# Projection of a hybrid layer: linear attention's levels in pairs, ten steps a chunk, queries scaled behind the eviction

## The chip, the cores and the metric

One core of one Trainium2 chip. The metric is the device time of one execution in microseconds (us). Engines: PE is TensorE (matmuls), PEld its weight loads, DVE is VectorE, ACT is ScalarE, POOL is GpSimd, SP is SyncE, which issues nearly all transfers. Each engine runs its own list of instructions in order, and semaphores order them against each other.

## What is computed

One decoder layer over 2048 prompt tokens and 8 x 8 sample tokens. Cut to what matters here:

```python
h = rms_norm(x, g_norm)
z = h @ w_in                       # the projection: 17 blocks of 512 columns
# forgetting attention on qa, ka, va; short convolution on xc, bc, cc, gc
# gated linear attention (GLA), 4 heads, key 64, value 128:
a = log_sigmoid(lrb @ w_gla_up + b_gla) / 16
b = cumsum(a)                      # within a chunk
att[t, s] = sum_d q[t, d] * k[s, d] * exp(b[t, d] - b[s, d])     # s <= t
o = (q * exp(b)) @ state + att @ v
state = exp(b_last) * state + (k * exp(b_last - b)).T @ v
out = x + merge(branches) @ w_out
```

The kernel computes this in four phases: the projection with GLA, the convolution and the forget sums woven into it (0 to about 1677 us of the span), attention of the prompt, attention of the samples, and merge with output projection.

## The kernel before

**Units.** The projection's matmuls are cut into 481 units. Units 17 to 480 go through 8 pairs of column blocks `j`; each pair takes 7 products `f` of sums and differences of operand blocks (so that 7 products do the work of 8), and each product takes 8 units `tp` of 12 matmuls of 128x512 into one of 3 buffers `z_ps`. After the 8 units of f = 0 and f = 4 comes one unit `sa` of 16 matmuls for the samples. PE starts unit u when unit u - 3 is evicted.

**What DVE does at unit u**, in this order: `split` (L1147: the low half of a weight slice for the next product, behind ACT's high half L969; at tp 2, 4, 6 and 7, L1147 is awaited by PE in the next product), `gla_steps(u)`, `product(u - 2)` (L1187, L1192, L1194; only for the blocks of j = 2 and 3), `evict(u)` (L1168 to L1175: one instruction, two for f = 5; f = 0 is evicted by ACT, L985). ACT: `split`, its GLA steps, `evict(u)`, the three activations of `sigmoid(u - 1)` (L1007 to L1011). POOL: `weight_sum` (L542 to L560), its GLA steps, one step of `convolve` (L568 to L574), none of which is tied to a unit's end except by data. PE: the unit, then its GLA step. SP: the loads of operands and weights, stores, its GLA step.

**GLA.** 16 prompt chunks of 128 tokens and one chunk of the 64 sample tokens (c = 16). Masks split the triangle of a chunk into 7 levels (3 for c = 16). For level i: POOL writes `dist` (L589, `distance`), ACT takes it to `dec` in two activations (L1044, L1049), DVE writes `qE` = queries times `dec` (L1266, two instructions), POOL writes `kE` (L597, `scale_keys`), PE multiplies them into `a_ps` (L1504, 4 matmuls, signals `paired`), DVE copies the level's blocks under a mask into `att` (L1213, `keep`, signals `kept`). `dist`, `dec`, `qE`, `kE` and `a_ps` have two buffers each, level n in buffer n % 2. PE's level n waits for `kept` of level n - 1.

**Steps.** `CHUNK_STEP` puts the steps of a chunk on units. `OPEN` lists the units of tp 0 to 6 from unit 52 on, without `sa`; a chunk takes 20 of them. Before, step s of chunk c lies at place 5 + 20c + 20s // 14 of that list, so steps are one or two places apart. Step -3: SP loads q, k, v. Step 0: PE turns them. Step 1: ACT and DVE make logits, the diagonal and the sum `cum` (about ten instructions). Step s has DVE's `qE` of level s - 2, PE's matmuls of level s - 3, DVE's `keep` of level s - 4. Step 9: `exp_b`, `q_in` (L1274), `k_out` (L1279). Step 10: PE turns `k_out`. Step 11: output matmuls (L1520, L1523), ACT copies `k_tok`. Step 12: `grow` (L1547). Step 13: `update` (L1220, four instructions) of the state. For c = 16, steps 12 to 19 take one sample each on PE (L1536, 8 matmuls; then, behind `wait_from(pe, state_ready, LAST + n)`, `grow`, 4 matmuls), and DVE's `update` of sample n is step 13 + n.

Of the kernel before, what the change touches and what calls it, by code (L numbers as in the profile page):

```python
# [163 lines left out]
def project(nc, arena, x_all, g_norm, w_main, w_tail, h_ops, z, tail_t, kv_out, g_gla, conv_w, state_conv, ext_prompt, ext_sample,  # L164
# [9 lines left out]
    LAST = TILES - 1  # L174
# [112 lines left out]
    PERIOD, BEHIND = 20, 5  # L287
    CHUNK_STEP = {}
    for c in range(TILES):
        for step in range(-3, 14 if c < LAST else 14 + DEC_BATCH):  # L290
            CHUNK_STEP.setdefault(OPEN[BEHIND + PERIOD * c + PERIOD * step // 14], []).append((c, step))
# [12 lines left out]
    with ExitStack() as stack:  # L304
# [182 lines left out]

        def level(c, i):
            return LEVELS * c + i
# [22 lines left out]
        def _(pool):  # L512
# [116 lines left out]
            for u in range(len(UNITS)):  # L629
# [6 lines left out]
                for c, step in CHUNK_STEP.get(u, []):  # L636
                    i = step - 2
                    if 0 <= i < len(halves_of(c)):
                        distance(c, i)
                        scale_keys(c, i)  # L640
                    elif step == 9:
                        distance(c, len(halves_of(c)))
# [5 lines left out]
        def _(sp):  # L648
# [142 lines left out]
            def gla(c, step):  # L791
                if step == -3:
# [11 lines left out]
                if step == (12 if c < LAST else 12 + DEC_BATCH):  # L804
# [14 lines left out]
                if c == LAST and step >= 14:  # L819
                    n = step - 14  # L820
# [103 lines left out]
        def _(act):  # L924
# [94 lines left out]
            def gla(c, step):  # L1019
                i = step - 2  # L1020
# [20 lines left out]
                elif 0 <= i < len(halves_of(c)):  # L1041
# [8 lines left out]
                elif step == 9:  # L1050
# [8 lines left out]
                elif step == 11:  # L1059
# [3 lines left out]
                if step == (12 if c < LAST else 12 + DEC_BATCH):  # L1063
# [55 lines left out]
        def _(dve):  # L1119
# [86 lines left out]
            def keep(c, i):  # L1206
                n = level(c, i)
                h = halves_of(c)[i]
                dve.wait_ge(paired, n + 1)
# [15 lines left out]
            def gla(c, step):  # L1225
                i = step - 2
# [31 lines left out]
                if 0 <= i - 2 < len(halves_of(c)):  # L1258
                    keep(c, i - 2)
                if 0 <= i < len(halves_of(c)):  # L1260
# [9 lines left out]
                elif step == 9:  # L1270
# [9 lines left out]
                if c < LAST and step == 13:  # L1280
# [3 lines left out]
                if c == LAST and 13 <= step < 13 + DEC_BATCH:  # L1284
                    n = step - 13
                    dve.wait_ge(grown, LAST + n + 1)
                    update(s_state[:, n], exp_b[:, :, (n + 1) * DEC_SEQ - 1])
                if c == LAST and 11 <= step < 11 + DEC_BATCH:
                    n = step - 11
# [53 lines left out]
            for u in range(len(UNITS) + 3):  # L1343
# [21 lines left out]
                gla_steps(u)  # L1365
# [3 lines left out]
                if u < len(UNITS):  # L1369
                    evict(u)  # L1370
                if u < TILES:
# [6 lines left out]
        def _(pe):  # L1378
# [106 lines left out]
            def gla(c, step):  # L1485
                i = step - 3
# [10 lines left out]
                elif 0 <= i < len(halves_of(c)):  # L1497
# [4 lines left out]
                    wait_from(pe, kept, n)  # L1502
# [4 lines left out]
                elif step == 10:  # L1507
# [6 lines left out]
                elif step == 11:  # L1514
# [12 lines left out]
                if c < LAST and step == 12:  # L1527
# [1718 lines left out]
```

## Time and profile before

| what | us |
|---|---|
| median of 3 runs (3643.61 to 3645.72) | 3643.92 |
| the profiled execution | 3641.52 |
| its span, first to last instruction | 3639.8 |
| PE busy in the span | 3415.4 (94%) |
| DVE, ACT, POOL busy in the span | 2193.9, 1797.8, 1653.6 |

The profile is of one execution. A row of a timeline is one instruction or a few equal ones (x4); what stands in square brackets is how long the engine had been idle and what it waited for. The spans of PE's matmuls are modelled and overlap: what counts is the distance of their starts.

### The profile page before, as it was taken

The page shows a single profiled execution, that of the slowest core. Times are in us where ns is not written, and L with a number is a line of the kernel's source. Part 1 is how long each engine was busy: PE and PEld are TensorE (multiplying, and loading weights), DVE is VectorE, ACT ScalarE, POOL GpSimd, SP SyncE. Part 2 cuts the span into 40 slices and gives each one's busy share as a digit, 9 for nine tenths or more (in the row PEclk, how much of TensorE's full clock was granted, in tenths as well). Part 3 has the DMA queues.
Part 4 walks back from the last instruction along what each step waited for, and adds up shares of the span by engine and source line. Part 5 has one row for each costly group of instructions (what it writes and reads, how often), then busy time and mean ns, then how long its engine had stood idle before and what let it go on. Part 6 is the DMA issues. An engine that isn't in the chain of part 4 may idle for free. (4 is left out here: it accounts for less than half of the span.)

```text
span 3639.8 us, 55125 instructions
## 1 busy us (share of the span) xinstructions
PE 3415.4 (94%) x17143; PEld 2675.7 (74%) x17143; DVE 2193.9 (60%) x3609; ACT 1797.8 (49%) x3707; POOL 1653.6 (45%) x1238
## 2 busy tenths in 40 slices
PE   7899999999999999997998998999999999899999
PEld 6678888777787778885666665777777776688787
DVE  4425456767665655554766663788888887544432
ACT  4411222544424464635676676777777776311222
POOL 1411314153535452211777775777777777222100
PEclk9999999999999999997999999999999999999999
DMA  7878787877888887885011113999999999544322
GB/s 269 321 231 287 211 281 235 300 254 247 277 304 295 269 264 239 260 233 167 13 36 47 30 42 109 318 331 333 331 330 336 334 333 314 194 159 159 136 93 78
DMA packets 430936, 818.82 MB, mean 225 GB/s; under 512 B 98449, under 2 KB 119865, under 8 KB 430670
## 3 DMA queue, kind: packets, MB, share of 16 engines
q1 hardware_dynamic: 418518, 808.32, 66.9%
q10 hardware_dynamic: 11584, 5.13, 0.5%
q8 instruction: 142, 2.33, 0.3%
q0 software_dynamic: 576, 2.10, 0.2%
q14 instruction: 116, 0.95, 0.1%
HBM read 674.12 MB, written 141.32 MB: 224 GB/s over the span
## 5 line engine op out<-in xcount | busy, mean ns | idle before, releaser
L1460 PE MATMUL prj_z_ps<-prj_w_hi,prj_h_ring 128*128 128x512 f32 x1792 | 725.7, 405 | 11.8 <-DMA prj_h_ring<-hops_scratch 7.2
L2381 POOL TENSOR_TENSOR sa_v_lo<-sa_v_raw,sa_v_hi 128x1024 fp32r<-128x1024 f32 x256 | 608.6, 2400 | 218.3 <-DVE sa_v_hi L2520 217.8
L1462 PE MATMUL prj_z_ps<-prj_w_hi,prj_h_ring 128*128 128x512 f32 x1792 | 704.9, 393 | 0.0
L1461 PE MATMUL prj_z_ps<-prj_w_lo,prj_h_ring 128*128 128x512 f32 x1792 | 703.3, 392 | 0.0
L1877 POOL TENSOR_TENSOR pa_p_lo<-pa_probs,pa_p_hi 128x512 fp32r<-128x512 f32 (+1 forms) x320 | 367.2, 1162 | 161.7 <-ACT pa_p_hi L1890 144.8
L2514 DVE TENSOR_TENSOR sa_kT_lo<-sa_t_ps,sa_kT_hi 128x512 fp32r<-128x512 f32 x512 | 345.3, 686 | 138.2 <-ACT sa_kT_hi L2403 134.9
L1460 PEld LDWEIGHTS prj_z_ps<-prj_w_hi,prj_h_ring 128*128 128x128 f32 x1792 | 340.4, 190 | 80.1 <-issue 8.0
L1462 PEld LDWEIGHTS prj_z_ps<-prj_w_hi,prj_h_ring 128*128 128x128 f32 x1792 | 339.3, 189 | 75.3
L1461 PEld LDWEIGHTS prj_z_ps<-prj_w_lo,prj_h_ring 128*128 128x128 f32 x1792 | 340.6, 190 | 66.7
L2403 ACT CAST sa_kT_hi<-sa_t_ps 128x512 fp32r<-128x512 f32 x512 | 291.6, 590 | 126.2 <-PE sa_t_ps L2667 119.1
L2667 PE MATMUL sa_t_ps<-arena_ident,arena_k_raw 128*128 128x128 f32 x2048 | 301.3, 278 | 26.7 <-DVE sa_kT_lo L2514 18.3
L2667 PEld LDWEIGHTS sa_t_ps<-arena_ident,arena_k_raw 128*128 128x128 f32 x2048 | 241.2, 141 | 107.3 <-DVE sa_kT_lo L2514 33.5
L589 POOL TENSOR_TENSOR prj_dist<-prj_cum 128x256 f32<-128x256 f32 x132 | 98.4, 746 | 380.5 <-DVE prj_cum L1256 380.5
L1919 ACT ACTIVATE pa_probs<-pa_st_ps 128x512 f32<-128x512 f32 (+1 forms) x320 | 171.1, 535 | 149.6 <-PE pa_st_ps L2124 72.6
L2014 DVE TENSOR_REDUCE pa_part_max<-pa_max_ps 128x1 f32<-128x512 f32 (+2 forms) x320 | 182.8, 603 | 103.1 <-PE pa_max_ps L2102 83.4
L1175 DVE TENSOR_TENSOR prj_z_sb<-prj_z_ps,prj_xy 128x512 f32<-128x512 f32 x192 | 132.3, 689 | 185.1 <-PE prj_z_ps L1462 183.9
L2730 PE MATMUL sa_o_ps<-sa_v_hi,sa_p_both 128*128 128x512 f32 x512 | 215.0, 420 | 9.0 <-POOL sa_v_lo L2381 5.9
L2673 PE MATMUL sa_s_ps<-sa_kT_hi,sa_q_both 128*128 128x512 f32 x512 | 212.6, 415 | 0.0
L597 POOL TENSOR_TENSOR prj_kE<-prj_kT,prj_dec 128x256 f32<-128x256 f32 x115 | 90.8, 790 | 254.6 <-ACT prj_dec L1049 197.3
L2731 PE MATMUL sa_o_ps<-sa_v_lo,sa_p_both 128*64 128x512 f32 x512 | 203.7, 398 | 0.0
L2674 PE MATMUL sa_s_ps<-sa_kT_lo,sa_q_both 128*64 128x512 f32 x512 | 202.2, 395 | 0.0
L2850 POOL TENSOR_TENSOR mo_merged<-mo_merged,arena_mg 128x1024 f32<-128x1024 f32 x34 | 81.8, 2406 | 243.6 <-DVE arena_mg L3052 243.6
(422 smaller groups left out, 7349.6 us busy)
## 6 DMA issues: line engine op xcount, KB each, us to landing
prj_h_ring<-hops_scratch SPq DMA_DIRECT2D x448, 512.0 KB, 4.6
arena_k_raw<-in_cache_k_dram SPq DMA_DIRECT2D x512, 256.0 KB, 4.1
sa_v_raw<-in_cache_v_dram SPq DMA_DIRECT2D x512, 256.0 KB, 4.3
z_scratch<-prj_z_sb SPq DMA_DIRECT2D x256, 256.0 KB, 5.4
prj_raw<-in_w_main_dram SPq DMA_DIRECT2D x104, 256.0 KB, 5.9
arena_mg<-z_scratch SPq DMA_DIRECT2D x51, 512.0 KB, 4.7
hops_scratch<-prj_h_ring SPq DMA_DIRECT2D x32, 512.0 KB, 5.8
arena_cu<-extp_scratch SPq DMA_DIRECT2D x48, 256.0 KB
```

The lines of the kernel that those rows point to most:

```text
L1460: pe.matmul(out, h[:, 0, k], hi, start=(k == 0), stop=False)
L1461: pe.matmul(out, h[:, 0, k], lo, start=False, stop=False)
L1462: mm = pe.matmul(out, h[:, 1, k], hi, start=False, stop=(k == HK - 1))
L1877: pool.tensor_tensor(p_lo[:, s % P_RING, 0:w], probs[:, s % P_RING, 0:w], p_hi[:, s % P_RING, 0:w].bitcast(F32), ALU.subtract).then_inc(pl ...
L2381: pool.tensor_tensor(v_lo[:, w % 2, at], v_raw[:, w % RING, at], v_hi[:, w % 2, at].bitcast(F32), ALU.subtract).then_inc(vlo_ready, 1)
L2403: act.copy(kT_hi[:, g % 2, :, j * PAGE:(j + 1) * PAGE], heads_of(t_ps[:, j % 2])).then_inc(khi_ready, 1)
L2514: dve.tensor_tensor(kT_lo[:, g % 2, :, at], heads_of(t_ps[:, j % 2]), kT_hi[:, g % 2, :, at].bitcast(F32), ALU.subtract).then_inc(klo_read ...
L2667: mm = pe.transpose(t_ps[:, j % 2, pair * PAGE:(pair + 1) * PAGE], k_raw[:, g % RING, j, pair * P:(pair + 1) * P], ident[:])
L2673: pe.matmul(out, q, hi(pair), start=(pair == 0), stop=False, skip_group_check=True)
L2674: mm = pe.matmul(out[0:R], q[:, 0:R], lo(pair), start=False, stop=(pair == PAIRS - 1), skip_group_check=True)
L2730: pe.matmul(out, p_both[:, slot, j], v_hi[:, slot, j], start=begin, stop=False, skip_group_check=True)
L2731: mm = pe.matmul(out[0:R], p_both[:, slot, j, 0:R], v_lo[:, slot, j], start=False, stop=end, skip_group_check=True)
```

## The change

Levels 2i and 2i + 1 share one step. A chunk has ten steps (0 to 9) that lie exactly two places of `OPEN` apart, and the loads step -2. The new helper `levels_at(c, step, lag)` gives the two levels of a step; DVE's `qE` has lag 2, PE's matmuls lag 3, `keep` lag 4. DVE calls `keep` right behind the splits of a unit and all its other GLA work behind `evict(u)`. PE's two levels of a step wait for `kept` of all levels before them, `keep` waits for `paired` of both levels of its step. `exp_b`, `q_in`, `k_out` come at step 5, the turn of `k_out` at 6, `k_tok` at 7, output matmuls and `grow` at 8, the `update` at 9. For c = 16, PE takes sample n at step 9 + n and DVE's `update` of sample n is step 10 + n; the last step is 18 (unit 479, before it was unit 473).

```diff
-    PERIOD, BEHIND = 20, 5
+    PERIOD, BEHIND, STEPS = 20, 5, 10
-        for step in range(-3, 14 if c < LAST else 14 + DEC_BATCH):
-            CHUNK_STEP.setdefault(OPEN[BEHIND + PERIOD * c + PERIOD * step // 14], []).append((c, step))
+        for step in range(-2, STEPS if c < LAST else 11 + DEC_BATCH):
+            CHUNK_STEP.setdefault(OPEN[BEHIND + PERIOD * c + PERIOD // STEPS * step], []).append((c, step))
...
+        def levels_at(c, step, lag):
+            return [i for i in (2 * (step - lag), 2 * (step - lag) + 1) if 0 <= i < len(halves_of(c))]
...
-                    i = step - 2
-                    if 0 <= i < len(halves_of(c)):
+                    for i in levels_at(c, step, 2):
                         distance(c, i)
+                    for i in levels_at(c, step, 2):
                         scale_keys(c, i)
-                    elif step == 9:
+                    if step == 5:
                         distance(c, len(halves_of(c)))
...
             def gla(c, step):
-                if step == -3:
+                if step == -2:
...
-                if step == (12 if c < LAST else 12 + DEC_BATCH):
+                if step == (9 if c < LAST else 9 + DEC_BATCH):
                     sp.wait_ge(o_ready, c + 1)
...
-                elif 0 <= i < len(halves_of(c)):
+                for i in levels_at(c, step, 2):
                     n = turn_of_dec(c, i)
                     act.wait_ge(apart, n + 1)
...
-                dve.wait_ge(paired, n + 1)
+                dve.wait_ge(paired, level(c, min(i // 2 * 2 + 2, len(halves_of(c)))))
...
-                if 0 <= i - 2 < len(halves_of(c)):
-                    keep(c, i - 2)
-                if 0 <= i < len(halves_of(c)):
+                for i in levels_at(c, step, 2):
                     n, h = level(c, i), halves_of(c)[i]
                     dve.wait_ge(dec_ready, turn_of_dec(c, i) + 1)
...
-                if c < LAST and step == 13:
+                if c < LAST and step == 9:
                     dve.wait_ge(grown, c + 1)
...
-                if c == LAST and 13 <= step < 13 + DEC_BATCH:
-                    n = step - 13
+                if c == LAST and 10 <= step < 10 + DEC_BATCH:
+                    n = step - 10
                     dve.wait_ge(grown, LAST + n + 1)
                     update(s_state[:, n], exp_b[:, :, (n + 1) * DEC_SEQ - 1])
...
-                gla_steps(u)
+                for c, step in CHUNK_STEP.get(u, []):
+                    for i in levels_at(c, step, 4):
+                        keep(c, i)
                 if u in FORGET_STEP:
                     forget(FORGET_STEP[u])
                 product(u - 2)
                 if u < len(UNITS):
                     evict(u)
+                gla_steps(u)
...
-                elif 0 <= i < len(halves_of(c)):
+                for i in levels_at(c, step, 3):
...
-                    wait_from(pe, kept, n)
+                    wait_from(pe, kept, level(c, i // 2 * 2))
...
-                elif step == 10:
+                if step == 6:
...
-                elif step == 11:
+                elif step == 8:
...
-                if c < LAST and step == 12:
+                if c < LAST and step == 8:
                     pe.wait_ge(ktok_ready, c + 1)
                     grow(k_tok[:], c)
-                if c == LAST and 12 <= step < 12 + DEC_BATCH:
-                    n = step - 12
+                if c == LAST and 9 <= step < 9 + DEC_BATCH:
+                    n = step - 9
```

## Rows read from the trace of the kernel before

**Rows 1.** Windows of the projection: length, busy PE, PEld, DVE, ACT, POOL, clock, DMA.
```profile
880.00:909.00 29.00, 23.64 (x104) 18.57 (x103) 27.25 (x44) 18.32 (x35) 10.13 (x11) 0.94 0.70 206
909.00:1375.00 466.00, 450.69 (x2102) 368.53 (x2102) 274.79 (x435) 211.58 (x411) 224.72 (x206) 0.99 0.83 280
...
1590.00:1650.00 60.00, 60.00 (x302) 50.59 (x302) 32.59 (x80) 31.27 (x52) 0.00 (x0) 1.00 0.83 229
```

**Rows 2.** Waits of the matmul engine, 300 to 1680: us, times, longest.
```profile
PE prj_a_ps L1504 <- DVE prj_att L1213: 31.1, 21, 4.7
PE prj_a_ps L1504 <- POOL prj_kE L597: 3.0, 2, 2.0
PE prj_z_ps L1460 <- DVE prj_w_lo L1147: 2.8, 1, 2.8
PE prj_z_ps L1460 <- DVE prj_xy L1173: 0.7, 1, 0.7
```

**Rows 3.** Timeline of the matmul engine around a level that waits for nothing.
```profile
719.71 0.39 PE L1462 MATMUL prj_z_ps<-prj_w_hi,prj_h_ring 128*128 128x512 f32 x1
719.94 0.60 PE L1504 MATMUL prj_a_ps<-prj_qE,prj_kE 128*128 128x128 f32 x4
720.30 0.48 PE L1460 MATMUL prj_z_ps<-prj_w_hi,prj_h_ring 128*128 128x512 f32 x1
720.62 0.40 PE L1461 MATMUL prj_z_ps<-prj_w_lo,prj_h_ring 128*128 128x512 f32 x1
```

**Rows 4.** Windows of low clock, first and last of six: PE busy, granted clock, DMA.
```profile
711.90:717.20 5.30, 5.30 (x15) 0.51 0.37 144
...
1362.20:1365.90 3.70, 3.70 (x12) 0.53 0.02 7
```

**Rows 5.** Timeline of the matmul engine: two waits, without and with a fall of the clock.
```profile
410.75 0.68 PE L1504 MATMUL prj_a_ps<-prj_qE,prj_kE 128*128 128x128 f32 x4 [2.11 <-DVE prj_att L1213]
...
982.91 0.76 PE L1504 MATMUL prj_a_ps<-prj_qE,prj_kE 128*128 128x128 f32 x4 [2.52 <-DVE prj_att L1213]
```

**Rows 6.** Timeline around 1358: start, us, engine, line, operation, idle before it.
```profile
1355.92 0.61 POOL L589 TENSOR_TENSOR prj_dist<-prj_cum 128x256 f32<-128x256 f32 x1
...
1356.57 0.42 ACT L1044 ACTIVATE prj_dist<-prj_dist 128x256 f32<-128x256 f32 x1 [3.64 <-POOL prj_dist L589]
...
1357.46 1.02 DVE L1266 TENSOR_TENSOR prj_qE<-prj_q_bd,prj_dec 64x128 f32<-64x128 f32 x2 [4.26 <-ACT prj_dec L1049]
...
1359.81 0.92 DVE L1147 TENSOR_TENSOR prj_w_lo<-arena_w_raw,prj_w_hi 128x512 fp32r<-128x512 f32 x1 [0.60 <-ACT prj_w_hi L969]
...
1360.66 0.71 DVE L1213 COPY_PREDICATED prj_att<-prj_masks,prj_a_ps 128x256 f32<-128x256 int32 x1
...
1361.52 1.20 PE L1504 MATMUL prj_a_ps<-prj_qE,prj_kE 128*128 128x128 f32 x4 [4.73 <-DVE prj_att L1213]
```

**Rows 7.** Timeline at a sample step, all engines.
```profile
1615.90 1.05 PE L1536 MATMUL prj_o_ps<-arena_x_in,prj_sig 128*128 128x128 f32 x8
...
1616.10 0.69 DVE L1175 TENSOR_TENSOR prj_z_sb<-prj_z_ps,prj_xy 128x512 f32<-128x512 f32 x1 [0.72 <-PE prj_z_ps L1462]
...
1616.71 0.68 DVE L1147 TENSOR_TENSOR prj_w_lo<-prj_raw,prj_w_hi 128x512 fp32r<-128x512 f32 x1
1616.79 1.03 PE L1547 MATMUL prj_g_ps<-prj_v_in,prj_k_seq 128*128 128x256 f32 x4
```

**Rows 8.** Timeline around 720: a `keep` that runs undisturbed.
```profile
720.77 0.43 DVE L1213 COPY_PREDICATED prj_att<-prj_masks,prj_a_ps 128x256 f32<-128x256 int32 x1
```

**Rows 9.** Timeline around 950: a split beside a sum on POOL.
```profile
949.61 1.35 POOL L542 TENSOR_TENSOR arena_w_raw<-prj_raw,arena_w_raw 128x512 f32<-128x512 f32 x1
...
949.83 1.68 DVE L1147 TENSOR_TENSOR prj_w_lo<-prj_raw,prj_w_hi 128x512 fp32r<-128x512 f32 x1
```

**Rows 10.** Timeline of VectorE: the second eviction of a unit of product 5.
```profile
902.52 0.68 DVE L1173 TENSOR_TENSOR prj_xy<-prj_z_ps,prj_xy 128x512 f32<-128x512 f32 x1
```

**Rows 11.** Timeline of VectorE just after rows 7.
```profile
1617.86 1.43 DVE L1220 SCALAR_TENSOR_TENSOR arena_x_in<-arena_x_in,prj_exp_b,prj_g_ps 64x128 f32<-64x128 f32 x4 [0.47 <-PE prj_g_ps L1547]
```

More of the change, by code:

```diff
@@ L818, in gla @@
                     sp.dma_start(view.rearrange("c p e -> p c e"), state[:]).then_inc(gla_stored, 16)
-                if c == LAST and step >= 14:
-                    n = step - 14
+                if c == LAST and step >= 11:
+                    n = step - 11
                     sp.wait_ge(state_ready, LAST + n + 1)
@@ L1019, in gla @@
             def gla(c, step):
-                i = step - 2
                 if step == 1:
@@ L1049, in gla @@
                     act.activation(dec[:, n % 2], dist[:, n % 2], ACT.Exp, scale=-INV_TAU).then_inc(dec_ready, 1)
-                elif step == 9:
+                if step == 5:
                     n = turn_of_dec(c, len(halves_of(c)))
@@ L1058, in gla @@
                     act.activation(dec[:, n % 2], dist[:, n % 2], ACT.Exp, scale=-INV_TAU).then_inc(dec_ready, 1)
-                elif step == 11:
+                elif step == 7:
                     act.wait_ge(k_turned, c + 1)
@@ L1062, in gla @@
                     act.copy(k_tok[:].rearrange("p c k -> p (c k)"), g_ps[:, 0:D_BK]).then_inc(ktok_ready, 1)
-                if step == (12 if c < LAST else 12 + DEC_BATCH):
+                if step == (9 if c < LAST else 9 + DEC_BATCH):
                     act.wait_ge(o_done, c + 1)
@@ L1225, in gla @@
             def gla(c, step):
-                i = step - 2
                 if c == 0 and step == 1:
@@ L1269, in gla @@
                     last.then_inc(qE_ready, 1)
-                elif step == 9:
+                if step == 5:
                     dve.wait_ge(expb_ready, c + 1)
@@ L1283, in gla @@
                     update(state, exp_b[:, :, P - 1])
-                if c == LAST and 13 <= step < 13 + DEC_BATCH:
-                    n = step - 13
+                if c == LAST and 10 <= step < 10 + DEC_BATCH:
+                    n = step - 10
                     dve.wait_ge(grown, LAST + n + 1)
                     update(s_state[:, n], exp_b[:, :, (n + 1) * DEC_SEQ - 1])
-                if c == LAST and 11 <= step < 11 + DEC_BATCH:
-                    n = step - 11
+                if c == LAST and 8 <= step < 8 + DEC_BATCH:
+                    n = step - 8
                     if n >= 2:
@@ L1485, in gla @@
             def gla(c, step):
-                i = step - 3
                 if step == 0:
@@ L1513, in gla @@
                     mm.then_inc(k_turned, 1)
-                elif step == 11:
+                elif step == 8:
                     pe.wait_ge(kept, level(c, len(halves_of(c)) - 1) + 1)
```

## The prediction

> **What bounds the kernel now.** I read the windows of the projection first, because the change touches nothing outside it. PE, the matmul engine, is busy 60.0 of 60 us where the sample steps lie, but 450.7 of 466 us from 909 to 1375 and 23.6 of 29 us from 880 to 909 [rows 1]. So the projection ends when PE has run its list, and any gap on PE adds to the time. DVE and POOL have room in the long window, with 275 and 225 of 466 us; from 880 to 909 DVE has none, with 27.25 of 29 us.
>
> The waits of PE say where the gaps are: 31.1 us in 21 waits of the level matmuls L1504 for DVE's `keep` (L1213), 3.0 us in 2 waits for `kE`, and 3.5 us on a split and an eviction [rows 2]. This idle time counts from the modelled end of a matmul, 0.39 us behind its start, while the next could start at 0.23 us [rows 3]: each of the 25 waits lost 0.16 us more, 4.0 us. Then the clock: behind six gaps PE ran at a granted clock of 0.51 to 0.54, the lower level of 1.2 GHz, for 3.5 to 5.3 us. Lost is length times (1 - clock): 2.6 us in the first such window, 1.7 us in the last, 11.7 us in all six [rows 4]. A gap of 2.11 us left the clock high, one of 2.52 us did not (clock 0.54 from 983.2 on) [rows 4, 5].
>
> The timeline around the longest gap shows the cause of the long ones. POOL was late with `dist`, ACT waited 3.64 us for it, DVE waited 4.26 us at `qE` for ACT, and only behind that came an eviction, a split and at last the `keep` on which PE stood for 4.73 us [rows 6]. `keep` had all it needed; it stood behind work that had not.
>
> **The change part by part.** *Order and distance of the levels.* PE's demand on `keep` no longer stands behind the `qE` of its unit: DVE runs its splits, then both `keep`s. Between PE's level steps lie at least two units, 2 x 12 matmuls 0.227 us apart [rows 3], 5.5 us. A delay at `qE` like that of 4.26 us would just fit. So 34.1 us of waits, 3.5 us on split and eviction, the 4.0 us beside them and 11.7 us of clock, 53.3 us, can go. What comes back stands in the next three parts.
>
> *Checkpoints that stay.* PE waits for `keep` at 49 places (steps 4, 5, 6 of 16 chunks, once for the samples) instead of 98. There DVE must start the eviction of the unit before (0.20 us after PE's next matmul, [rows 7]), run it (0.61 us until the next instruction), run the split if the unit has one (0.65), two `keep`s (0.4 each, [rows 8]), and 0.15 us pass until PE starts (the `keep` of 1360.66 ended at 1361.37, PE started at 1361.52, [rows 6]): 2.4 us against a unit of 2.7 us. At 28 places without a split 1.0 us is to spare, at 21 with one 0.3 us. A split beside a POOL instruction took 1.68 us [rows 9], which makes a gap of 0.7 us. Bounds: 0 if every split runs alone, 15 us if all 21 meet POOL. POOL is busy half the time [rows 1], and ACT's half of a split can be late too, as by 0.60 us at 1359.81 [rows 6]: I take 9 us.
>
> *Where DVE is full.* In product 5 of GA and GB (877 to 910) a unit brings DVE two evictions, two products and half a split. From the end of unit 233 to the `keep` of unit 238 that is 5 x 2 evictions and 4 x 2 products at 0.61 (a product has an eviction's shape), 2 splits at 0.68, 6 `keep`s at 0.4 [rows 8], three levels of `qE` at 1.02, and `q_in` with `k_out` at 1.3 (an estimate, from `qE`'s and `keep`'s rows) [rows 6, 7, 10]: 19.1 us, and 0.2 us before the start. PE needs 5 x 2.72 us for its units and 1.6 us for four levels, 15.2 us. So 4.1 us of gap are left, with one fall of the clock, 1.7 us [rows 4]. At unit 182, where a split was 2.8 us late [rows 2], the order is nearly as before; I leave 2.2 us. Together 8 us. Bounds: 4, and 20 if all of today's gaps there and their clock stay.
>
> *Fewer interruptions of PE.* A level's 4 matmuls take 0.36 us of PE, and the second matmul behind them starts 0.32 instead of 0.23 us after the first [rows 3]. Per prompt chunk the stops go from 11 to 6: levels pair up, the turn of `k_out` joins the last level, `grow` joins the output matmuls. With one less in the last chunk that is 81 stops at 0.09 us, -7.3 us. Bounds 0 and -7.3.
>
> *The update of the sample states.* This is the price of the order. PE's `grow` of sample n waits for the `update` of sample n - 1, and both belong to the same step, before and after. Before, DVE ran the `update` ahead of the eviction, while PE was still in the unit: no wait, 60.0 of 60 us busy [rows 1]. Now it stands behind `evict(u)`, which waits for the end of the unit. From the start of the 8 sample matmuls (1615.90): the eviction starts at +0.20 and takes until +0.81 [rows 7], `update` lasts 1.43 us [rows 11], 0.15 us to PE [rows 6]: +2.39. PE is ready for `grow` at +0.89 [rows 7]. So 1.50 us of gap, and 0.60 us more in product 5 with its second eviction [rows 10]. Seven samples (n = 1 to 7) pay, at units 460, 462, 473, 475 (products 4 and 6) and 466, 468, 470 (product 5): 4 x 1.50 + 3 x 2.10 = 12.3 us. The unit that hid it is gone as a cover. Bounds 10 and 14 us, and 5 us more (3 x 1.7) if the gaps of 2.1 us make the clock fall.
>
> *At nothing.* Steps 1, 5 and 9 on DVE behind the eviction: at most some ten instructions that PE wants two units later. ACT's two levels (four activations at 0.42, 1.7 us [rows 6]) stand in front of its eviction and sigmoid, which have the three buffers of `z_ps` to cover them; without cover it is that 1.7 us at a step. SP issues the loads of a chunk 4 places ahead instead of 5, 11 us before PE turns them, and waits for the copy of `o_sb` in the same unit as before. The last sample state is stored from unit 479 of 480, and the last gate block leaves later.
>
> **Sum**, against the profiled execution's own 3641.5 us: -53.3 - 7.3 + 9 + 8 + 12.3 = -31.3, 3610.2 us. The median of the runs lies 2.4 us above the profiled one, so 3613 us.
>
> **Rivals.** *Slower: masks behind contended splits.* If each of the 49 checkpoints comes 1.1 us late (a contended split, 0.7, and ACT's half late besides), they cost 54 us instead of 9: 3658 us. It decides from (60.6 - 20.3) / 49 = 0.82 us a checkpoint on. For it: the split of 1.68 us and the wait of 0.60 us [rows 6, 9]. Against it: 28 of the places have no split. The Trainium skill, "SBUF — State Buffer", section "Who interferes with whom", has a rule that speaks for this rival: a VectorE instruction with two SBUF inputs and a GpSimd one that reads SBUF want the same read interface, and the later one waits for all of the earlier. The trace agrees: 1.68 us beside a sum of 1.35 us that had started 0.22 us before [rows 9]. By the rule alone, 21 splits held by up to those 1.35 us would cost up to 28 us where the sum has 9: an estimate of 3632 us.
>
> *No change that shows:* the same at 0.7 us a checkpoint (34 us), with the clock falling in the sample gaps (17.3 us) and 8 us where DVE is full: 59.3 of 60.6 us come back, 3643 us.
>
> *More gain:* PE finds each `keep` ready, and DVE's full stretch drains into the units around it; only 12.3 us come back: 3641.5 - 60.6 + 12.3 + 2.4 = 3596 us. Against it: 27.25 of 29 us [rows 1].
>
> *The order does nothing for the waits on `keep`,* because the real delay is POOL's: 34.1 + 3.7 + 11.7 us stay, 11.1 go, 12.3 come: 3645 us. For it: POOL heads the chain [rows 6]. Against it: a level is now wanted two units after its step, and POOL has half its time free [rows 1].
>
> **How the numbers follow.** Forecast 0.66, more gain 0.10, no change that shows 0.10, slower by the splits 0.08, POOL's delay stays 0.06. A difference under 0.2% (7.3 us) I take as one that this measurement can't tell from none. Faster 0.76: the first two. Same 0.13: the third and half of the last. Slower 0.11. The range goes from the better case, 3596, to 3643, the mildest of the bad ones. By the bounds of its terms the forecast alone holds 3600 to 3631.
>
> **What would show it.** In the changed profile: L1504's waits for L1213 fall from 31.1 to 10 to 15 us, none over 3 us outside 870 to 910; windows of low clock from six to one or two; seven waits in front of L1547, none before, of 1.3 to 2 us, between units 460 and 475; DVE idles at L1266 no longer ahead of an eviction. The prediction is wrong if the `keep`s come late at most places with a split, if gaps of 2.1 us cost the clock, or if ACT's longer steps delay its splits.

## The result and the profile after

| | median, us | runs | ratio to before |
|---|---|---|---|
| before | 3644.82 (3643.61 to 3649.41) | 4 | |
| after | 3685.89 (3681.74 to 3687.40) | 4 | 1.0109, interval 1.0097 to 1.0122 |

The change made the kernel 41 us slower. Forecast was 3613 us, and the range ended at 3643. The profiled execution's span grew from 3639.8 to 3685.1 us, PE's busy time from 3415.4 to 3423.9 us only: the new time is mostly time in which PE stands. Nearly all of it (43.2 of 45.3 us) is in the projection, whose last matmul into `z_ps` starts at 1720.6 us of the span instead of at 1677.4.

The windows of the projection in the kernel after, columns as in [rows 1]:

```profile
880.00:909.00 29.00, 19.42 (x77) 14.78 (x75) 25.69 (x35) 15.67 (x30) 13.86 (x13) 0.82 0.57 191
909.00:1375.00 466.00, 443.74 (x2072) 362.74 (x2072) 293.54 (x440) 205.35 (x401) 217.20 (x201) 0.99 0.82 277
...
1590.00:1650.00 60.00, 57.31 (x275) 47.67 (x274) 28.40 (x55) 18.87 (x33) 6.86 (x6) 1.00 0.75 212
```

PE lost in each: 4.2 us more around 880 to 909, 7 us more in the long window, and 2.7 us in a stretch that had been full. (The windows lie at the same times, not at the same units, since the kernel after runs behind.) Over the whole span DVE has the same 3609 instructions and is busy 2231.3 us instead of 2193.9, which is the first sign that they had become longer.

The waits of PE in the kernel after, 300 to 1740 us (us, times, longest), against [rows 2]:

```profile
PE prj_a_ps L1505 <- DVE prj_att L1215: 40.2, 27, 3.9
PE prj_g_ps L1548 <- DVE arena_x_in L1222: 11.1, 7, 1.9
...
PE prj_z_ps L1462 <- DVE prj_w_lo L1149: 9.8, 7, 3.5
PE prj_z_ps L1480 <- DVE prj_w_lo L1149: 6.7, 1, 6.7
```

Half the checkpoints on `keep` are gone, and yet PE stands longer there than before (40.2 against 31.1 us); the sample waits are the seven that the prediction announced; and a third kind has grown, waits on the splits, from 2.8 to 16.5 us. The waits of this view leave out restarts and slow clock, so I made a second account from the starts of the matmuls. For each I took the distance to the next start, less the distance that the same two kinds of matmul have when nothing disturbs them, and put the rest down to the matmul that came late. From the timelines of PE, 300 us to the end of the projection, this gives (us):

| | before a level | before a projection matmul | in slow clock | at sample steps | sum |
|---|---|---|---|---|---|
| before | 37.8 | 3.3 | 15.6 | 7.1 | 63.8 |
| after | 44.5 | 21.1 | 22.1 | 19.3 | 107.0 |

The difference of the sums is 43.2 us, and by as much is the last `z_ps` matmul later.

Why a `keep` comes late shows around 432 in the kernel after, a stretch with a checkpoint of step 6. Timeline; start, us, engine, line, operation, idle before it:

```profile
432.47 1.46 DVE L1265 TENSOR_TENSOR prj_qE<-prj_q_bd,prj_dec 64x128 f32<-64x128 f32 x2
...
433.74 5.63 POOL L563 TENSOR_TENSOR prj_raw<-prj_raw 128x512 f32<-128x512 f32 x4
...
433.95 2.84 DVE L1273 TENSOR_TENSOR prj_q_in<-prj_q_bd,prj_exp_b 64x256 f32<-64x256 f32 x2
...
436.83 1.40 DVE L1278 TENSOR_TENSOR prj_k_out<-prj_kT,prj_dec 128x256 f32<-128x256 f32 x1
438.16 0.68 DVE L1170 TENSOR_TENSOR prj_xy<-prj_z_ps,prj_xy 128x512 f32<-128x512 f32 x1
438.76 1.15 DVE L1149 TENSOR_TENSOR prj_w_lo<-arena_w_raw,prj_w_hi 128x512 fp32r<-128x512 f32 x1
439.83 1.27 DVE L1215 COPY_PREDICATED prj_att<-prj_masks,prj_a_ps 128x256 f32<-128x256 int32 x2
...
441.25 0.68 PE L1505 MATMUL prj_a_ps<-prj_qE,prj_kE 128*128 128x128 f32 x4 [3.06 <-DVE prj_att L1215]
```

Step 5 leaves DVE a bundle behind its eviction: the last level's `qE`, `q_in` and `k_out`. POOL meanwhile runs four sums of 1.4 us each. From 432.47 to 438.16 DVE works 5.7 us on five small instructions, and the next unit's eviction, split and `keep` (step 6) come behind them. PE stands 3.06 us. DVE never waited for data here: it was held inside its instructions.

How far that goes is seen where product 5 fills DVE, in the kernel after:

```profile
881.91 4.31 POOL L571 TENSOR_TENSOR arena_cu<-arena_cu,arena_taps 128x512 f32<-128x512 f32 x3
...
883.01 4.69 DVE L1265 TENSOR_TENSOR prj_qE<-prj_q_bd,prj_dec 64x128 f32<-64x128 f32 x4
...
890.26 0.68 DVE L1149 TENSOR_TENSOR prj_w_lo<-prj_raw,prj_w_hi 128x512 fp32r<-128x512 f32 x1
...
891.00 0.79 PE L1480 MATMUL prj_z_ps<-prj_w_hi,prj_hs 128*128 128x512 f32 x1 [6.71 <-DVE prj_w_lo L1149]
```

Four `qE` in a row take 4.69 us while POOL runs its convolution steps back to back, and the next unit's two products and eviction push the split on which PE waits 6.71 us to 890.26. Where POOL is idle the same four are done in 1.19 us:

```profile
715.52 1.19 DVE L1265 TENSOR_TENSOR prj_qE<-prj_q_bd,prj_dec 64x128 f32<-64x128 f32 x4
```

Rows of the stretch from 883 on with one instruction each show how the 4.69 us come about:

```profile
883.62 1.33 POOL L571 TENSOR_TENSOR arena_cu<-arena_cu,arena_taps 128x512 f32<-128x512 f32 x1
...
883.81 1.28 DVE L1265 TENSOR_TENSOR prj_qE<-prj_q_bd,prj_dec 64x128 f32<-64x128 f32 x1
...
884.89 1.32 POOL L571 TENSOR_TENSOR arena_cu<-arena_cu,arena_taps 128x512 f32<-128x512 f32 x1
...
885.12 1.24 DVE L1265 TENSOR_TENSOR prj_qE<-prj_q_bd,prj_dec 64x128 f32<-64x128 f32 x1
```

The two `qE` end at 885.09 and 886.36, 0.14 and 0.15 us behind POOL's 884.95 and 886.21. The first and the fourth do the same (883.79 behind 883.65, 887.70 behind 887.55). So each `qE` is held until POOL's current instruction is done, and the next one meets the next of POOL's. Over the projection (180 to 1735 us), DVE's groups of before and then of after, busy us and mean ns of one, idle time behind the second bar:

```profile
L1266 DVE TENSOR_TENSOR prj_qE<-prj_q_bd,prj_dec 64x128 f32<-64x128 f32 x230 | 129.5, 563 | 65.5 <-ACT prj_dec L1049 63.6
...
L1274 DVE TENSOR_TENSOR prj_q_in<-prj_q_bd,prj_exp_b 64x256 f32<-64x256 f32 x34 | 24.0, 705 | 0.2
```

```profile
L1265 DVE TENSOR_TENSOR prj_qE<-prj_q_bd,prj_dec 64x128 f32<-64x128 f32 x230 | 158.9, 691 | 30.2 <-ACT prj_dec L1051 17.7 <-PE prj_a_ps L1505 9.2
...
L1273 DVE TENSOR_TENSOR prj_q_in<-prj_q_bd,prj_exp_b 64x256 f32<-64x256 f32 x34 | 32.1, 944 | 0.7
```

The same 230 `qE` grew from 563 to 691 ns, the same 34 `q_in` from 705 to 944 ns: 37.5 us more of DVE in two lines. The idle time of `qE` behind ACT fell, as the prediction wanted, from 63.6 to 17.7 us; DVE's order did what it should there, but in place of that idle time stands time inside instructions.

The Trainium skill, "SBUF — State Buffer", section "Who interferes with whom", says that a VectorE instruction with two SBUF inputs contends with a GpSimd one that reads SBUF, and calls the port pair that they share an exclusive lock. The rows at 883.01 and 715.52 agree (4.69 and 1.19 us).

### The profile page after: what moved, and what is told of

Read it like the earlier page. It is cut to its first block and busy times, and to the rows that moved or that the text cites. A ratio compares the mean times of both kernels' runs of the same rounds, so it can differ in the third digit from the quotient of the medians.

```text
span 3685.1 us, 55124 instructions
## 1 busy us (share of the span) xinstructions
PE 3423.9 (93%) x17143; PEld 2680.2 (73%) x17143; DVE 2231.3 (61%) x3609; ACT 1794.3 (49%) x3707; POOL 1653.1 (45%) x1238
## 5 line engine op out<-in xcount | busy, mean ns | idle before, releaser
L1265 DVE TENSOR_TENSOR prj_qE<-prj_q_bd,prj_dec 64x128 f32<-64x128 f32 x230 | 158.9, 691 | 30.2 <-ACT prj_dec L1051 17.7
```

## The experiments

Each kernel's time is a median, with the kernel before run on the same chip. A kernel whose name begins with a is the changed one with an edit, one with b the kernel before with an edit.

### The update of the sample states ahead of the eviction (a_update_ahead)

```diff
                     for i in levels_at(c, step, 4):
                         keep(c, i)
+                    update_sample(c, step)     # the block for c == LAST, moved out of gla()
                 ...
                     evict(u)
                 gla_steps(u)
```

> The changed kernel with one edit: for c = 16, DVE runs the update of a sample behind the keeps and ahead of the eviction. The seven waits in front of grow (11.1 us in the rows, 12.2 with 0.16 us each beside them) go: 3674 us, by every theory. If the update ahead holds up its evictions, less than 5 us is gained.

3667.66 us (3662.72 to 3670.32), before 3644.37, ratio 1.0068 (1.0051 to 1.0085). The seven waits on L1222 are gone, the waits on splits stay as they were (16.6 us), and those on `keep` nearly so:

```profile
PE prj_a_ps L1508 <- DVE prj_att L1215: 38.5, 26, 3.4
```

By the ratios 15 us, by the medians 18 us of the 41 belong to the sample updates, more than the 12 that I had expected. Some 23 to 26 us belong to something else.

### `q_in` one step later (a_qin_later)

```diff
-                if step == 5:
+                if step == 6:
                     dve.wait_ge(expb_ready, c + 1)
                     ...                                # q_in, two instructions
+                if step == 5:
                     n = turn_of_dec(c, len(halves_of(c)))
                     ...                                # k_out
```

> The changed kernel with q_in (two DVE instructions, 0.94 us each) at step 6 instead of step 5. Theory A, the bundle of step 5 (qE of level 6, q_in, k_out) behind the eviction makes DVE late for the keeps of step 6: the waits of L1505 at step 6 (some 29 of 44 us) fall to under 10, the clock rises, 3655 us (gain 25 to 35). Theory B, any DVE work behind the eviction runs beside POOL and is late: the wait moves elsewhere, gain under 8 us. Theory C, two levels in one step are what is late: gain under 8 us.

3667.06 us (3665.58 to 3670.27), ratio 1.0065 (1.0048 to 1.0082): 16 us by the ratios, 19 by the medians. That is between what theory A wanted (25 to 35) and what B and C allowed (under 8).

```profile
PE prj_a_ps L1506 <- DVE prj_att L1215: 31.3, 25, 3.5
...
L1273 DVE TENSOR_TENSOR prj_q_in<-prj_q_bd,prj_exp_b 64x256 f32<-64x256 f32 x34 | 18.5, 544 | 0.2
```

Two instructions a chunk moved one step, and PE's waits on `keep` fell by 8.9 us (the first row) and its slow clock by 7.4 us (22.1 to 14.7 in the working above). So step 5's bundle is a real part of it, and not all. `q_in` also got shorter where it stands now, 544 against 944 ns: what it costs depends on what POOL does beside it.

### Queries ahead of the eviction again (a_queries_ahead)

```diff
                         keep(c, i)
+                gla_steps(u)
                 ...
                     evict(u)
-                gla_steps(u)
```

> The changed kernel with all GLA work of DVE ahead of product and eviction again (keeps still first): steps in pairs alone. If the place behind the eviction is what costs (theories A and B): the sample waits go (-12) and the waits of step 6 and of the splits shrink, 3635 to 3650 us, near the kernel before. If two levels in one step are what costs (theory C): 3670 to 3680, only the 12 us of the samples gained.

3688.48 us (3685.49 to 3691.00), ratio 1.0120 (1.0103 to 1.0137).

```profile
PE prj_a_ps L1505 <- DVE prj_att L1215: 50.1, 29, 5.5
...
L1265 DVE TENSOR_TENSOR prj_qE<-prj_q_bd,prj_dec 64x128 f32<-64x128 f32 x230 | 149.2, 649 | 87.9 <-PE prj_a_ps L1505 62.7 <-ACT prj_dec L1051 21.5
```

This is slower than both of my forecasts for it (3635 to 3650 and 3670 to 3680). It is the pairing of the levels without the move of the queries, and it has no sample waits: pairs and ten steps alone cost 44 us. Given the pairs, the move behind the eviction gains 19 to 21 us: that is the distance from here to a_update_ahead, which has the move and also no sample waits.

The second row shows something that I had not thought of. A `qE` of level n overwrites the buffer of level n - 2, so with two levels in a step DVE must wait until PE has multiplied both levels of the step before, and PE does that at the end of the same unit. Ahead of the eviction DVE stands 62.7 us for it; behind the eviction it is 9.2 us (the row of `qE` after, above). So pairs that share two buffers want the queries behind the eviction.

### The order in the kernel with fourteen steps (b_behind)

```diff
-                if 0 <= i - 2 < len(halves_of(c)):
-                    keep(c, i - 2)
...
-                gla_steps(u)
+                for c, step in CHUNK_STEP.get(u, []):
+                    if 0 <= step - 4 < len(halves_of(c)):
+                        keep(c, step - 4)
                 ...
                     evict(u)
+                gla_steps(u)
```

> The kernel before with its 14 steps, keeps first and all other GLA work of DVE behind the eviction: order alone. If the place costs (A and B): slower than before by 25 us or more (12 for the samples, the rest at the step with q_in and k_out and at splits), 3670 to 3700. If the pairing costs (C): 12 us for the samples and some gain from the order, 3640 to 3657.

3675.41 us (3671.93 to 3678.06), ratio 1.0088 (1.0071 to 1.0105): 31 us slower than before.

```profile
PE prj_a_ps L1505 <- DVE prj_att L1213: 39.8, 22, 6.1
```

The seven sample waits are there as in the kernel after (11.0 us), so some 15 to 18 of the 31 us are theirs. The rest is waits on `keep`, longer than before's (39.8 against 31.1 us). PE names `keep` in all of them and `qE` in none. The longest is the chain of [rows 6] again, only with the eviction ahead of `qE`: POOL's sums hold up `dist`, ACT comes late with `dec` and then with its half of the next split, and `keep` stands behind that split.

```profile
796.37 0.62 POOL L589 TENSOR_TENSOR prj_dist<-prj_cum 128x256 f32<-128x256 f32 x1
...
797.92 1.02 DVE L1264 TENSOR_TENSOR prj_qE<-prj_q_bd,prj_dec 64x128 f32<-64x128 f32 x2 [2.03 <-ACT prj_dec L1049]
...
800.26 0.69 DVE L1147 TENSOR_TENSOR prj_w_lo<-arena_w_raw,prj_w_hi 128x512 fp32r<-128x512 f32 x1 [1.32 <-ACT prj_w_hi L969]
...
801.46 0.55 PE L1505 MATMUL prj_a_ps<-prj_qE,prj_kE 128*128 128x128 f32 x1 [6.08 <-DVE prj_att L1213]
```

That is one wait; how much of the rest has this cause was not tested by itself.

Along one path of kernels the parts are: pairs +44, the order given the pairs -21, sample updates +18, together +41. (They add up because each kernel differs from the next in one part; with 14 steps the order had another price.) That tells which part, not yet by which mechanism.

### Queries read from PSUM (a_q_psum, b_q_psum)

If DVE's instructions are held by POOL because both their inputs are in SBUF, one input in PSUM should free them. The first bank of `t_ps` has no other use while GLA runs:

```diff
-        q_bd = m.sb("q_bd", [P, PAIRS, 2, P])
+        q_bd = t_ps[:, 0].rearrange("p (c h t) -> p c h t", h=2, t=P)
...
-        GLA_FILLED = 5
+        GLA_FILLED = 4
...
-                    for x in (q_bd, q_in, state, att, qE):
+                    for x in (q_in, state, att, qE):
```

> The changed kernel with the scaled queries q_bd in a PSUM bank that is free during GLA (t_ps), instead of SBUF. The work and the order are the same, but each qE and q_in instruction of DVE has one SBUF input instead of two. Theory D, DVE's SBUF-and-SBUF instructions wait out POOL's (four qE in a row took 4.69 us beside POOL's convolution, 1.19 us without): the means of qE (691 ns) and q_in (944 ns) fall to about 300 and 600 to 700 ns, DVE busy falls by 80 us or more, and the waits of PE for keeps and splits (61 us in the rows) fall by more than half: 3640 to 3655 us. If the stalls come from POOL being late with dist (theory E): the DVE means fall too, but PE's waits do not, gain under 10 us.

> The kernel before with the same one edit, q_bd in PSUM. Theory D: its 34 us of level waits fall less than those of the changed kernel, since only one level's qE meets POOL at a time: 3625 to 3638 us, so the distance to the changed kernel with this edit is 25 us or less instead of 41. Theory E: within 5 us of before, and the distance stays 35 or more.

a_q_psum: 3654.67 us (3644.38 to 3658.66, 10 runs), ratio 1.0020 (1.0008 to 1.0031). b_q_psum: 3633.80 us (3630.10 to 3640.60, 10 runs), ratio 0.9969 (0.9960 to 0.9979). In a_q_psum DVE's group and PE's waits:

```profile
L1265 DVE TENSOR_TENSOR prj_qE<-prj_t_ps,prj_dec 64x128 f32<-64x128 f32 x230 | 66.0, 287 | 36.4 <-ACT prj_dec L1051 20.4 <-PE prj_a_ps L1505 12.9
...
PE prj_a_ps L1505 <- DVE prj_att L1215: 19.4, 13, 3.2
```

And the place of product 5 in its timeline, where four `qE` run beside an instruction of POOL:

```profile
883.84 1.21 DVE L1265 TENSOR_TENSOR prj_qE<-prj_t_ps,prj_dec 64x128 f32<-64x128 f32 x4
...
883.98 1.30 POOL L574 TENSOR_TENSOR arena_cu<-arena_cu 128x512 f32<-128x512 f32 x1
```

`qE` is 287 ns in the one and 286 ns in the other, down from 691 and 563: half of it before, and more than half after, was waiting for POOL. It is not shorter for being in PSUM: with POOL idle it was as short in SBUF (1.19 us for four). PE's waits on `keep` fall from 40.2 to 19.4 us, and with those on splits from 56.7 to 31.1 us, a fall of 45% where I had expected over half. The edit is worth 31 us in the changed kernel and 11 us in the kernel before; the distance between the two kernels falls from 41 to 21 us, and 15 to 18 of these are the sample updates. The edit also frees `q_in` (944 to 422 ns), so the 31 and 11 us are of `qE` and `q_in` together. The Trainium skill's section named above also says that a VectorE instruction with at most one SBUF input, outside its 2-port modes, doesn't contend; four `qE` in 1.21 us beside POOL's L574 agree.

### All three mended, and the order with fourteen steps (a_three, b_order_q_psum)

a_three is the changed kernel with the update ahead, `q_in` at step 6 and the queries in PSUM. b_order_q_psum is b_behind with the sample update ahead of the eviction and the queries in PSUM.

> The changed kernel with three edits together: sample updates ahead of the eviction (gave 18 us alone), q_in one step later (19 us alone), q_bd in PSUM. If they add up with theory D: 3610 to 3630 us, faster than before. If pairs of levels cost what they cost whatever their inputs: 3645 to 3655.

> The kernel before, 14 steps, with keeps first, the sample updates ahead of the eviction, the other GLA work behind it, and q_bd in PSUM. Order without pairs and without contended queries. Theory D: 3610 to 3630 us. If the place behind the eviction costs by itself (it cost 31 us with 14 steps, of which 12 to 18 are the samples): 3640 to 3655.

a_three: 3638.29 us (3634.08 to 3642.59, 10 runs), ratio 0.9980 (0.9970 to 0.9989). b_order_q_psum: 3645.05 us (3640.41 to 3652.54, 10 runs), ratio 1.0000 (0.9990 to 1.0009). The three edits, 18, 19 and 31 us one by one, give 48 us together and not 68: presumably `q_in` later and queries in PSUM take away the same waits in part. a_three hit neither of its two forecasts (3610 to 3630 and 3645 to 3655), and b_order_q_psum refutes the 3610 to 3630 that theory D gave for it. With all three edits the changed kernel is a little faster than before. It isn't faster than b_q_psum, which has the old schedule and one of the three edits (4.5 us by the medians, with intervals that overlap). With the queries in PSUM the order alone costs 11 us (b_q_psum to b_order_q_psum), and PE's waits on `keep` go from 21.1 to 30.2 us:

```profile
PE prj_a_ps L1508 <- DVE prj_att L1213: 30.2, 14, 6.2
```

Much of what is left in a_three has another cause. PE waits for `keep` 14 times there, 22.7 us in all. In 7 of them, with 13.1 us, DVE's `keep` stood behind a split that had waited 1.4 to 3.0 us for ACT's high half. The longest:

```profile
1353.19 0.60 ACT L972 CAST prj_w_hi<-arena_w_raw 128x512 fp32r<-128x512 f32 x1
...
1353.82 1.20 DVE L1149 TENSOR_TENSOR prj_w_lo<-arena_w_raw,prj_w_hi 128x512 fp32r<-128x512 f32 x1 [2.43 <-ACT prj_w_hi L972]
...
1356.37 0.55 PE L1509 MATMUL prj_a_ps<-prj_qE,prj_kE 128*128 128x128 f32 x1 [3.55 <-DVE prj_att L1215]
```

The prediction had named ACT's delay of its splits as a sign of being wrong. In the kernel after it stands in front of only 4 of the 27 late `keep`s (delays of 0.9 to 1.4 us, in waits of 8.7 of the 40.2 us). No run moved ACT's work, so what it costs is not tested.

### POOL's long instructions cut short (a_small_pool, b_small_pool)

Both leave work out: the sums of weight blocks after the first pair and the convolution's steps treat 8 of 512 columns. The instructions, their order and their semaphores stay.

```diff
-                    pool.tensor_tensor(w_raw[:, k], raw2[:, 0, k], w_raw[:, k], ALU.subtract)
+                    pool.tensor_tensor(w_raw[:, k, 0:8], raw2[:, 0, k, 0:8], w_raw[:, k, 0:8], ALU.subtract)
...
-                    pool.tensor_tensor(cu[r, step], cu[r, step], taps[r, step], ALU.mult)
+                    pool.tensor_tensor(cu[r, step, 0:8], cu[r, step, 0:8], taps[r, step, 0:8], ALU.mult)
```

> The changed kernel with POOL's weight sums (after the first pair of blocks) and its convolution cut to 8 of 512 columns; they are the work left out, and the order and all waits stay. POOL's 1.3 us instructions shrink, so nothing long is left on POOL beside DVE but dist and kE. Theory D with POOL as the cause of most stalls: PE's waits for keeps and splits fall from 61 us to under 15, 3620 to 3635 us, what is left being the 18 us of the samples. If pairs and order make DVE late by themselves: over 3650 us.

> The kernel before with the same parts left out. POOL as the cause: its waits fall too, 3600 to 3612 us, and the distance to the changed kernel with this edit is the sample updates, 15 to 22 us. Otherwise the distance stays near 41.

a_small_pool: 3628.32 us (3626.59 to 3631.85), ratio 0.9964 (0.9950 to 0.9978). b_small_pool: 3607.89 us (3606.58 to 3610.47), ratio 0.9905 (0.9889 to 0.9922). Both times lie in the range of POOL as the cause. The waits on `keep` of the one and of the other:

```profile
PE prj_a_ps L1505 <- DVE prj_att L1215: 12.2, 12, 3.2
```

```profile
PE prj_a_ps L1504 <- DVE prj_att L1213: 9.2, 7, 2.6
```

This takes away both things that POOL can do to the levels, its hold on DVE and its own lateness. Before gains 35 us by it, after 53 (by the ratios) to 58 us (by the medians), and their distance is 20 us again: the sample updates and little more. With POOL's long instructions gone the new schedule still gains nothing over the old one, so the waits that it was to remove go back mostly to POOL (31.1 us on `keep` in the kernel before, 9.2 without POOL's long instructions). The edit leaves `kE` and `dist` whole, and `qE` still has a mean of 544 ns in the one and 443 ns in the other beside them. It comes to the same distance as queries in PSUM by another way, which supports the share given there; it can't part POOL's hold from POOL's lateness.

### Distances ahead of the weight sums (a_dist_first, b_dist_first)

The rival that POOL is late with `dist` [rows 6], tested by POOL's order. a_dist_first is a_three with it, b_dist_first is b_q_psum with it:

```diff
             for u in range(len(UNITS)):
+                for c, step in CHUNK_STEP.get(u, []):
+                    if 0 <= step - 2 < len(halves_of(c)):
+                        distance(c, step - 2)
                 for x in SUMS_AT.get(u, []):
                     weight_sum(*x)
                 ...
-                        distance(c, i)
                         scale_keys(c, i)
```

> The changed kernel with sample updates ahead, q_in later, q_bd in PSUM, and on POOL the two dist of a unit ahead of its weight sums instead of behind. If the waits that are left (25 for keeps, 15 for splits) come from late dist: 3618 to 3630 us. If they come from DVE's splits beside POOL: within 4 us of the 3638 without this edit.

> The kernel before with q_bd in PSUM and POOL's dist ahead of the weight sums. The chain POOL, ACT, qE, eviction, split, keep was the cause of its long gaps: with dist 2.6 us earlier most of the 30 us of waits go, 3605 to 3622 us. If within 4 us of the 3634 without this edit, the chain is held up elsewhere (convolution, ACT).

a_dist_first: 3633.32 us (3628.91 to 3638.95, 7 runs), ratio 0.9971 (0.9960 to 0.9983): 3 to 5 us better than a_three, with intervals that overlap. b_dist_first: 3619.96 us (3614.24 to 3623.85, 4 runs; before 3643.38), ratio 0.9934 (0.9918 to 0.9951): 13 to 14 us better than b_q_psum. PE's waits in it, where b_q_psum had 21.1 us on `keep` and 6.7 on `kE`:

```profile
PE prj_a_ps L1506 <- DVE prj_att L1215: 10.7, 12, 2.4
PE prj_a_ps L1506 <- POOL prj_kE L597: 6.0, 3, 2.6
```

In the kernel before, POOL's lateness was worth as much as the contention, and both go without any new schedule. This version beats both kernels, by 0.7% and 1.8%.

### Pairs with the queries in PSUM (a_ahead_q_psum, a_ahead_dist_first)

a_queries_ahead with the queries in PSUM, and that with the distances ahead of the sums.

> The changed kernel with DVE's GLA work ahead of product and eviction (3688 us alone) and q_bd in PSUM. If the pairs cost because four qE in a row meet POOL: 3645 to 3655 us. If they cost because DVE stands at qE for a late dist in front of its evictions: over 3668 us.

> The same with POOL's two dist ahead of the weight sums. If the late dist is the rest of the cost: 10 us or more under a_ahead_q_psum. If the rest is DVE's splits, products and k_out beside POOL: within 5 us of it.

a_ahead_q_psum: 3646.32 us (3643.39 to 3649.51, 10 runs), ratio 1.0004 (0.9995 to 1.0014). a_ahead_dist_first: 3646.31 us (3637.89 to 3650.04, 10 runs), ratio 0.9998 (0.9988 to 1.0007).

```profile
PE prj_a_ps L1505 <- DVE prj_att L1215: 28.9, 20, 3.7
```

The 44 us that pairs cost fall to nothing against the kernel before, and to 13 us against b_q_psum (1.0004 less 0.9969). So 31 of the 44 us go with the hold on the queries, which is longer where four `qE` stand in a row than where two do (`q_in` is in it too). POOL's order adds nothing here. DVE still stands for PE ahead of `qE` as in a_queries_ahead (65.8 us against 62.7), so those waits for the two buffers are worth at most the 13 us that are left.

## Why the prediction was wrong

Two steps of it failed. It took the length of DVE's queries as fixed, though it was in good part a wait for POOL that grew with the new order, so the 53.3 us of *Order and distance of the levels* never came. And it put the bundle of step 5 at nothing.

**At nothing: steps 1, 5 and 9 behind the eviction.** I counted instructions and asked when PE wants their results, two units later. I didn't ask what stands behind them on DVE: the next unit's eviction, split and `keep`, and PE wants that `keep`. Of the 27 checkpoints that made PE wait, 14 were those of step 6, the `keep`s behind step 5's bundle, with 24.0 of the 40.2 us (the "29 of 44" in my expectation of a_qin_later was too high). One piece of the bundle moved a step on gave 16 to 19 us back (a_qin_later). It isn't the place behind the eviction that makes this cost: in a_queries_ahead the bundle stands ahead of the eviction, and the 14 checkpoints of step 6 cost 28.5 us. It is that `q_in` and `k_out` now come with a level's `qE` one step ahead of a checkpoint. Before, they came at step 9 behind that step's `keep` and without a `qE`.

**The price of `qE`.** This is the step with the most weight. I took 1.02 us for a level's two [rows 6] as if it were their length. It is 0.57 us (2 x 0.286, b_q_psum) and the rest was POOL. The trace of before had shown it, in rows that I didn't put side by side:

```profile
727.51 0.58 DVE L1266 TENSOR_TENSOR prj_qE<-prj_q_bd,prj_dec 64x128 f32<-64x128 f32 x2
...
799.89 2.02 DVE L1266 TENSOR_TENSOR prj_qE<-prj_q_bd,prj_dec 64x128 f32<-64x128 f32 x2
```

The price of a held instruction goes with what POOL does at that moment and with how many short ones stand in a row, so it was no constant to carry to the new order: it went from 563 to 691 ns. With the hold on the queries taken away the changed kernel gained 31 us and the kernel before 11, so this step has some 20 of the 41 us, and the sample updates most of the rest. (The 16 to 19 us of `q_in` above are in part the same time, since `q_in` is held too.) It is the main reason why *Order and distance of the levels* failed. Of its 53.3 us, the 37.8 us lost in front of levels became 44.5, the 3.3 us in front of projection matmuls 21.1, and slow clock went from 15.6 (where the prediction had counted 11.7) to 22.1 us. Its mechanism exists: `qE`'s idle time behind ACT fell by 46 us, and given the pairs the order was worth 19 to 21 us. It was outweighed by what the pairs cost. Without the pairs the order gained nothing: there it cost 11 us with the queries in PSUM.

**Checkpoints that stay**, 9 us with bounds 0 and 15. I let the splits alone be held, by 0.7 us at most. All that DVE runs between two `keep`s with two SBUF inputs can be held: `qE`, `q_in`, `k_out` and products as well. The evictions, which read PSUM, took 0.69 us in both kernels. Among the prices that I gave, this one was mis-sized most: of the 44.5 us in front of levels I had planned 9, and the few more where DVE is full.

**Where DVE is full**, 8 us with an upper bound of 20. One split there cost 6.71 us by itself, and from 880 to 909 PE was busy 19.4 of 29 us with a clock of 0.82: 4.2 us less of busy time than before, at a lower clock too. The contended `qE` of 4.69 us, which I had in at 2.04 us, is in it.

**Fewer interruptions of PE**, -7.3 us with 0 as a bound: the bound was right. In the kernel after, a double level that waits for nothing:

```profile
722.63 1.05 PE L1505 MATMUL prj_a_ps<-prj_qE,prj_kE 128*128 128x128 f32 x8
723.44 0.48 PE L1462 MATMUL prj_z_ps<-prj_w_hi,prj_h_ring 128*128 128x512 f32 x1
723.75 0.40 PE L1463 MATMUL prj_z_ps<-prj_w_lo,prj_h_ring 128*128 128x512 f32 x1
```

Eight matmuls take 0.81 us and the second one behind them starts 0.31 us after the first: 0.81 + 0.31 - 0.23 is 0.89 us, and two single levels are 2 x (0.36 + 0.32 - 0.23), 0.90 us [rows 3]. In these rows the 0.09 us go with each four small matmuls, not with each stop.

**The update of the sample states**, 12.3 us: right in place, number and size. Two of the seven, in the kernel after:

```profile
1640.92 1.10 PE L1548 MATMUL prj_g_ps<-prj_v_in,prj_k_seq 128*128 128x256 f32 x4 [1.32 <-DVE arena_x_in L1222]
...
1684.28 1.34 PE L1548 MATMUL prj_g_ps<-prj_v_in,prj_k_seq 128*128 128x256 f32 x4 [1.92 <-DVE arena_x_in L1222]
```

4 x 1.32 and 3 x 1.92 make 11.0 us of idle time, and 7 x 0.16 more 12.2 us. Behind the wait at 1684.28 the clock fell, as the upper bound had it (a window in the last section). Taken away, it gave 15 to 18 us.

**The sum's own range.** The prediction says that the forecast alone holds 3600 to 3631 by the bounds of its terms. Added up, these bounds (-7.3 to 0, 0 to 15, 4 to 20, 10 to 19) give 3597 to 3645. That doesn't reach 3686 either: the miss lies in the 53.3 us, which had no bound, and in the step at nothing.

**The rivals.** *Masks behind contended splits*, 3658 us at 0.08, was nearest: right mechanism, right rule, but it counted only splits. *POOL's delay stays* named something true of the kernel before (13 to 14 us in b_dist_first), though in a_three it was worth at most 3 to 5 us. What I lacked was a case in which all of DVE's two-input instructions are held. Of the signs I had named, the seven sample waits and the vanished idle time came; waits on `keep` of 10 to 15 us came as 40.2, "none over 3 us outside 870 to 910" is refuted by the 3.06 us at 441.25, and the windows of low clock in the projection went from six to ten, not to one or two.

**What stays open.** The remaining distance once samples and held queries are out is 3 to 4 us between a_q_psum and b_q_psum (21 less 18 by the medians), which is within what the intervals leave. Splits, products and `k_out` still have two SBUF inputs in every run, and no run freed them by themselves. ACT's late half of the splits, which leads most of the waits left in a_three, was not tested. Whether a ten-step schedule could be tuned below b_dist_first was not tried. The share of the slow clock can't be parted from the waits that bring it about: no run changed one without the other.

## What to carry to other kernels

When instructions are moved or put together in one step, ask what then stands behind them on their own engine, and let PE's next demand on that engine decide, not only the demand on their results. The mean duration of a short VectorE instruction with two SBUF inputs in a trace with a busy GpSimd is no price: take its shortest undisturbed row as its length and the rest as a wait that grows when several stand in a row. If one operand can live in a free PSUM bank, do that first; here it was worth more than the new schedule.

## What the runs showed of the hardware

- More than half of `qE`'s time in the kernel after (287 of 691 ns is its length) and half before (286 of 563 ns) was the hold by POOL. Four of 0.3 us took 4.69 us beside POOL instructions run back to back, each ending 0.14 to 0.15 us behind one of POOL's. They took 1.19 us beside an idle POOL, and 1.21 us with the queries in PSUM beside a POOL instruction of 1.30 us.
- `q_in` read from PSUM took 422 ns instead of 944 (a_q_psum), and in SBUF 544 ns at another place (a_qin_later).
- A gap of 1.92 us on PE was followed by a fall of the clock once, and two others of 1.92 us were not. The windows of the kernel after ahead of the wait at 1684.28 and behind it (columns as in [rows 1]):

```profile
1680.00:1684.00 4.00, 2.36 (x15) 1.93 (x13) 2.52 (x7) 3.54 (x6) 0.00 (x0) 1.00 0.95 263
...
1685.80:1687.60 1.80, 1.80 (x6) 1.37 (x5) 0.00 (x0) 0.00 (x0) 0.00 (x0) 0.50 0.93 304
```

  The granted clock of 0.50 is the lower level, 1.2 GHz, and matmuls start 0.43 us apart there. In [rows 5] a gap of 2.11 us left the clock high, so the length of the gap alone doesn't tell which one it is.
